# Stick-breaking attention inside an input projection: suffix sums with rounded fp32 operands in two parts, and another order of the step's matrix products

## What is computed

```python
z = einsum('bhqd,bhkd->bhqk', q, k) * scale
log_fail = where(before, log_sigmoid(-z), 0.0)          # before: key < query
later = cumsum(log_fail, axis=3, reverse=True) - log_fail
log_a = log_sigmoid(z) + later
a = where(before, exp(where(before, log_a, 0.0)), 0.0)
out = einsum('bhqk,bhkd->bhqd', a, v)
```

## Time and profile before

| | |
|---|---|
| median of 3 runs | 2329.61 us (2328.22 to 2335.32) |
| profiled execution, own time | 2328.99 us |
| its span, first to last instruction | 2327.3 us |
| PE busy | 2208.1 us, 95% |
| DVE, ACT, POOL busy | 1124.9, 855.8 and 417.6 us |
| mean granted TensorE clock | 0.964 |

### The profile page before, as it was taken

One profiled execution on the slowest core, in us unless ns is written; L12 is line 12 of the kernel. 1 busy time (PEld: TensorE's weight loads), 2 busy tenths in 40 slices (PEclk: granted clock), 3 DMA queues, 4 the chain that ended last, 5 costly groups with the idle time before them and its releaser, 6 DMA issues. The chain is left out here.

```text
span 2327.3 us, 29119 instructions
## 1 busy us (share of the span) xinstructions
PE 2208.1 (95%) x10778; PEld 1772.1 (76%) x10778; DVE 1124.9 (48%) x1810; ACT 855.8 (37%) x1407; POOL 417.6 (18%) x461
## 2 busy tenths in 40 slices
PE   7999999999889999998899989999999997999988
PEld 6888887766667888887788878886778887876657
DVE  5444324423436444324475544337656784655443
ACT  4322223443334322223432232135446743433453
POOL 2111002113333111001120010001100341014441
PEclk8999999999989999999899999999999997999999
DMA  4333333511022333331333246740243220242202
GB/s 136 115 92 98 93 100 84 95 46 55 19 73 73 108 91 99 91 99 52 103 98 90 82 76 108 98 80 1 73 119 82 55 55 20 76 97 60 52 19 67
DMA packets 359321, 182.10 MB, mean 78 GB/s; under 512 B 41926, under 2 KB 356015, under 8 KB 358831
## 3 DMA queue, kind: packets, MB, share of 16 engines
q1 hardware_dynamic: 359214, 180.69, 30.6%
HBM read 176.14 MB, written 4.52 MB: 78 GB/s over the span
## 5 line engine op out<-in xcount | busy, mean ns | idle before, releaser
L313 PE MATMUL ps<-xh,wh 128*128 128x512 f32 x1920 | 768.3, 400 | 12.9 <-DVE wl L280 10.9
L315 PE MATMUL ps<-xh,wl 128*128 128x512 f32 x1920 | 750.7, 391 | 0.0
L314 PE MATMUL ps<-xl,wh 128*128 128x512 f32 x1920 | 750.0, 391 | 0.0
L280 DVE TENSOR_TENSOR wl<-raw,wh 128x1024 fp32r<-128x1024 f32 x334 | 422.7, 1267 | 437.4 <-ACT wh L270 432.6
L270 ACT ACTIVATE wh<-raw 128x1024 fp32r<-128x1024 f32 x334 | 342.1, 1027 | 363.9 <-PE ps L315 332.6
L313 PEld LDWEIGHTS ps<-xh,wh 128*128 128x128 f32 x1920 | 361.9, 188 | 104.2 <-issue 18.2
L315 PEld LDWEIGHTS ps<-xh,wl 128*128 128x128 f32 x1920 | 361.6, 188 | 77.6
L314 PEld LDWEIGHTS ps<-xl,wh 128*128 128x128 f32 x1920 | 362.4, 189 | 73.6 <-issue 2.4
L457 PE MATMUL ps<-xh,wh 128*128 128x512 f32 x304 | 132.2, 435 | 26.2 <-ACT xh L392 15.5
L450 POOL TENSOR_TENSOR acc<-acc,sq 128x512 f32<-128x512 f32 x72 | 102.4, 1423 | 275.9 <-ACT sq L835 178.0
L314 PE MATMUL ps<-a_lo,wh 128*128 128x512 f32 x352 | 137.0, 389 | 0.0
(11 more groups left out here) (379 smaller groups left out, 2527.4 us busy)
## 6 DMA issues: line engine op xcount, KB each, us to landing
raw<-in_w_ffn_gate SPq DMA_DIRECT2D x44, 512.0 KB, 3.8
raw<-in_w_ffn_up SPq DMA_DIRECT2D x44, 512.0 KB, 3.8
raw<-in_w_ffn_down SPq DMA_DIRECT2D x32, 512.0 KB, 3.6
raw<-in_conv_w_in SPq DMA_DIRECT2D x32, 512.0 KB, 4.0
raw<-in_fox_w_in SPq DMA_DIRECT2D x32, 512.0 KB, 9.6
raw<-in_gdn_w_in SPq DMA_DIRECT2D x32, 512.0 KB, 4.1
raw<-in_w_in SPq DMA_DIRECT2D x24, 512.0 KB, 3.8
raw<-in_swa_w_in SPq DMA_DIRECT2D x32, 256.0 KB, 3.8
```

The source lines that it names most:

```text
L280: nc.vector.tensor_tensor(wl[s][:, 0:kb, :], raw[r][:, 0:kb, :], wh[s][:, 0:kb, :].bitcast(F32), ALU.subtract).then_inc(lo_done, 1)
L313: pe.matmul(o, wh[s][:, kb, :], x_hi, start=start, stop=False)
L314: pe.matmul(o, wh[s][:, kb, :], x_lo, start=False, stop=False)
L315: return pe.matmul(o, wl[s][:, kb, :], x_hi, start=False, stop=stop)
```

## The change

The softplus matrix is kept as two fp32r tensors, `softplus_hi` (rounded by ACT) and `softplus_lo` (the rest, by DVE), and `tri` becomes fp32r too. Each suffix product is then issued twice, once for each part. ACT's rounding comes after the exponential of the unit before; DVE's subtraction, `sb_rest`, stands ahead of the next step of the unit: within a tile right ahead of it, else at the start of the next tile that has a step, ahead of that tile's `wl`. On PE the sums over later blocks come first, once `sp_raw` says that z has been read, then the value product of unit s-2, and last the triangle, once the unit's own parts are there (`sp_parts`). `weights` gets two buffers of one unit each.

```diff
-            tri = sb("tri", [P, 2, P], ctx=c)
+            tri = sb("tri", [P, 2, P], F32R, ctx=c)
...
-            SP_ = sb("softplus", [P, 2, wide], ctx=c)
-            A = sb("weights", [P, 2, wide], ctx=c)
+            sp_hi = sb("softplus_hi", [P, 2, wide], F32R, ctx=c)
+            sp_lo = sb("softplus_lo", [P, 2, wide], F32R, ctx=c)
+            A = sb("weights", [P, 4, SEQ], ctx=c)
...
+            def sb_t(u, w):
+                return tmp[:, 2 * (u % 2):2 * (u % 2) + 2, 0:w]
+            def sb_a(u, w):
+                return A[:, 2 * (u % 2):2 * (u % 2) + 2, 0:w]
...
+                def suffix(u, k2):
+                    kb = sb_units[u][1]
+                    for r in range(2):
+                        for part in (sp_hi, sp_lo):
+                            m = pe.matmul(sb_z(u)[:, r, (k2 - kb) * P:SEQ - kb * P], ntri if k2 == kb else nones,
+                                          part[:, r, off[k2]:off[k2] + SEQ - k2 * P],
+                                          start=False, stop=True, skip_group_check=True)
+                    return m
                 if 1 <= s < SU + 1:
                     u = s - 1
-                    kb, z = sb_units[u][1], sb_z(u)
                     if u == 0:
                         pe.wait_ge(sbc, 2)
-                    pe.wait_ge(sp_d, u + 1)
-                    for r in range(2):
-                        for k2 in range(kb, TB):
-                            m = pe.matmul(z[:, r, (k2 - kb) * P:SEQ - kb * P], ntri if k2 == kb else nones,
-                                          SP_[:, r, off[k2]:off[k2] + SEQ - k2 * P],
-                                          start=False, stop=True, skip_group_check=True)
-                    m.then_inc(c_mm, 1)
+                    pe.wait_ge(sp_raw, u + 1)
+                    for k2 in range(TB - 1, sb_units[u][1], -1):
+                        suffix(u, k2)
                 if 2 <= s < SU + 2:
                     u = s - 2
                     pair, kb = sb_units[u]
...
                     pe.wait_ge(a_d, u + 1)
                     for r in range(2):
                         pe.matmul(ps[OUT][HD * r:HD * r + HD, kb * P:SEQ], v_cols(pair % 3, kb, r),
-                                  A[:, r, off[kb]:off[kb] + SEQ - kb * P],
+                                  sb_a(u, SEQ - kb * P)[:, r, :],
                                   start=kb == 3, stop=kb == 0, skip_group_check=True).then_inc(av_mm, 1)
+                if 1 <= s < SU + 1:
+                    u = s - 1
+                    pe.wait_ge(sp_parts, u + 1)
+                    suffix(u, sb_units[u][1]).then_inc(c_mm, 1)
...
-                    kb = sb_units[s][1]
-                    w = SEQ - kb * P
-                    dve.wait_ge(ln_d, s + 1)
-                    if s >= 4:
-                        dve.wait_ge(c_mm, s // 4 * 4)
-                    nc.vector.scalar_tensor_tensor(out=SP_[:, :, off[kb]:off[kb] + w], in0=sb_z(s),
-                                                   scalar=0.0, in1=tmp[:, 2 * (s % 2):2 * (s % 2) + 2, 0:w], op0=ALU.max,
+                    w = SEQ - sb_units[s][1] * P
+                    dve.wait_ge(ln_hi, ln_of(s))
+                    nc.vector.scalar_tensor_tensor(out=sb_t(s, w), in0=sb_z(s), scalar=0.0, in1=sb_t(s, w), op0=ALU.max,
                                                    op1=ALU.add).then_inc(sp_raw, 1)
+            def sb_rest(dve, u):
+                kb = sb_units[u][1]
+                w = SEQ - kb * P
+                o = off[kb]
+                dve.wait_ge(ln_hi, hi_of(u))
+                nc.vector.tensor_tensor(sp_lo[:, :, o:o + w], sb_t(u, w), sp_hi[:, :, o:o + w].bitcast(F32),
+                                        ALU.subtract).then_inc(sp_parts, 1)
+            def ln_of(u):
+                return 2 * u + 1
+            def hi_of(u):
+                return 2 * u + 2
...
-                    t = tmp[:, 2 * (s % 2):2 * (s % 2) + 2, 0:w]
+                    t = sb_t(s, w)
                     act.wait_ge(z_mm, 2 * s + 2)
                     if s >= 2:
-                        act.wait_ge(sp_raw, s - 1)
-                    nc.scalar.activation(t, sb_z(s), ACT.Abs).then_inc(abs_d, 1)
-                    act.wait_ge(abs_d, s + 1)
-                    nc.scalar.activation(t, t, ACT.Exp, scale=-1.0).then_inc(exp_d, 1)
-                    act.wait_ge(exp_d, s + 1)
-                    nc.scalar.activation(t, t, ACT.Ln, bias=1.0).then_inc(ln_d, 1)
+                        act.wait_ge(sp_parts, s - 1)
+                    nc.scalar.activation(t, sb_z(s), ACT.Abs).then_inc(abs_exp, 1)
+                    act.wait_ge(abs_exp, 2 * s + 1)
+                    nc.scalar.activation(t, t, ACT.Exp, scale=-1.0).then_inc(abs_exp, 1)
+                    act.wait_ge(abs_exp, 2 * s + 2)
+                    nc.scalar.activation(t, t, ACT.Ln, bias=1.0).then_inc(ln_hi, 1)
                 if 1 <= s < SU + 1:
                     u = s - 1
-                    kb = sb_units[u][1]
                     act.wait_ge(c_mm, u + 1)
-                    if u >= 4:
-                        act.wait_ge(av_mm, u // 4 * 8)
-                    nc.scalar.activation(A[:, :, off[kb]:off[kb] + SEQ - kb * P], sb_z(u), ACT.Exp).then_inc(a_raw, 1)
-
-            def sb_pool(pool, s):
-
+                    if u >= 2:
+                        act.wait_ge(av_mm, 2 * u - 2)
+                    nc.scalar.activation(sb_a(u, SEQ - sb_units[u][1] * P), sb_z(u), ACT.Exp).then_inc(a_raw, 1)
                 if s < SU:
                     kb = sb_units[s][1]
-                    v = SP_[:, :, off[kb]:off[kb] + P]
+                    act.wait_ge(sp_d, s + 1)
+                    if s >= 4:
+                        act.wait_ge(c_mm, s // 4 * 4)
+                    nc.scalar.activation(sp_hi[:, :, off[kb]:off[kb] + w], t, ACT.Copy).then_inc(ln_hi, 1)
...
+            def steps_of_sb(k):
+                return [s for kind, s in act_at(k) if kind == "s"]
+            def dve_between(dve, i, j, part):
+                at = steps_of_sb(4 * i + j)
+                if part == 1 and at and 1 <= at[0] < SU + 1:
+                    sb_rest(dve, at[0] - 1)
             def dve_amid(dve, k):
                 for kind, s in act_at(k):
+                    if kind == "s" and s != steps_of_sb(k)[0] and 1 <= s < SU + 1:
+                        sb_rest(dve, s - 1)
                     dve_do(dve, kind, s)
...
-                nc.gpsimd.memset(nones, -1.0).then_inc(sbc, 1)
+                nc.gpsimd.memset(nones.bitcast(F32), -1.0).then_inc(sbc, 1)
...
-            in_proj("mix_in", gains("g_mix_pre"), None, update=half[:, 0, :], evac_dve=mix_evac,
+            in_proj("mix_in", gains("g_mix_pre"), None, update=half[:, 0, :], evac_dve=mix_evac, between_dve=dve_between,
```

More of the change, by code:

```diff
@@ L1297, in kernel_program @@
                 "sq", "sum", "mm", "ms", "inv", "root", "spread", "rstd", "f"))
-            (sbc, z_mm, abs_d, exp_d, ln_d, sp_raw, sp_d, c_mm, a_raw, a_d, av_mm, o_d) = (sem(f"sb_{x}") for x in (
-                "const", "z", "abs", "exp", "ln", "spraw", "sp", "c", "araw", "a", "av", "o"))
+            (sbc, z_mm, abs_exp, ln_hi, sp_raw, sp_d, sp_parts, c_mm, a_raw, a_d, av_mm, o_d) = (sem(f"sb_{x}") for x in (
+                "const", "z", "absexp", "lnhi", "spraw", "sp", "parts", "c", "araw", "a", "av", "o"))
             ntri, nones = tri[:, 0, :], tri[:, 1, :]
@@ L1370, in sb_act @@
                     w = SEQ - sb_units[s][1] * P
-                    t = tmp[:, 2 * (s % 2):2 * (s % 2) + 2, 0:w]
+                    t = sb_t(s, w)
                     act.wait_ge(z_mm, 2 * s + 2)
                     if s >= 2:
-                        act.wait_ge(sp_raw, s - 1)
-                    nc.scalar.activation(t, sb_z(s), ACT.Abs).then_inc(abs_d, 1)
-                    act.wait_ge(abs_d, s + 1)
-                    nc.scalar.activation(t, t, ACT.Exp, scale=-1.0).then_inc(exp_d, 1)
-                    act.wait_ge(exp_d, s + 1)
-                    nc.scalar.activation(t, t, ACT.Ln, bias=1.0).then_inc(ln_d, 1)
+                        act.wait_ge(sp_parts, s - 1)
[4 more added lines that the diff above has]
+                    nc.scalar.activation(t, t, ACT.Ln, bias=1.0).then_inc(ln_hi, 1)
                 if 1 <= s < SU + 1:
                     u = s - 1
-                    kb = sb_units[u][1]
                     act.wait_ge(c_mm, u + 1)
-                    if u >= 4:
-                        act.wait_ge(av_mm, u // 4 * 8)
-                    nc.scalar.activation(A[:, :, off[kb]:off[kb] + SEQ - kb * P], sb_z(u), ACT.Exp).then_inc(a_raw, 1)
+                    if u >= 2:
+                        act.wait_ge(av_mm, 2 * u - 2)
+                    nc.scalar.activation(sb_a(u, SEQ - sb_units[u][1] * P), sb_z(u), ACT.Exp).then_inc(a_raw, 1)
+                if s < SU:
+                    kb = sb_units[s][1]
+                    act.wait_ge(sp_d, s + 1)
+                    if s >= 4:
+                        act.wait_ge(c_mm, s // 4 * 4)
```

(11 more changed lines are left out.)

## The result

The changed kernel takes 2316.36 us (median of 5 runs, 2314.38 to 2319.34), the kernel before in the same comparison 2329.74 us (5 runs, 2328.22 to 2335.32). The medians differ by 13.4 us; the ratio is 0.9945 with a 95% interval of 0.9935 to 0.9956, so 0.55% less. The forecast was 2318.0 us, 11.6 us less, in a range of 2314.5 to 2324.5. The profiled execution took 2315.31 us, its span is 2313.6 us.

What follows compares the result with a forecast made beforehand. PE's own work was taken to bound the sixteen units. 12.8 us saved on suffix records, less waits of 0.5, 0.4 and 0.3, gave 11.6 us off the 2329.61 median: 2318.0 us, stated range 2314.5 to 2324.5.

Steps and rivals of the forecast that it cites:

- Part 1: Suffix sums on PE: 160 records in fp32r instead of fp32, cheaper from 256 columns on, save 12.8 us.
- no gain below 512 columns: Bound on the suffix records: narrow fp32r products cost the same as fp32 records, leaving 3.2 us saved.
- the flat 0.11 up to 384 columns: Bound on the suffix records: 0.11 us each at 384 and 256 columns too, 15.2 us saved.
- second: Rival, suffix products: narrow fp32r products gain nothing; 3.2 us saved less 1.2, 2327.6 us; chance 0.05.
- third: Rival, suffix products: a narrow fp32r product costs a whole fp32 product of its width; 10.5 us slower, 2340; chance 0.05.
- fourth rival: Suffix products: narrow ones cost columns alone, 0.057 us at 128; 16.4 us saved less 1.2, 2314.4; chance 0.03.
- Part 2: New order on PE: same number of shape changes except in four steps; 0 to 0.4 us gained, taken as 0.
- Part 3: Sixteen roundings on ACT and subtractions on DVE fit in idle time; triangle waits for both, unit 11 cover 0.2 us.
- The two losses: PE waits: 0.5 us at unit 0's triangle, 0.4 us at the transposition behind step 2.
- The fifth rival: Time is given back behind the units, in the banded part or later; 2324 to 2329 us; chance 0.03.
- the longer chain: First rival: ACT, DVE and hand-overs take longer than walked, the triangle waits; 2321 or 2327 us; chance 0.10.

Runs made afterwards that it cites:

- the order alone: Kernel before with only PE's new order, all fp32 in one tensor, no roundings or subtractions: 2326.60 us against 2327.42, ratio 0.9997.
- the parts alone: Changed kernel with all suffix products of a unit behind the wait for `softplus_lo` and ahead of the value product: 2325.29 us, ratio 0.9985.
- the second comparison: Changed kernel run again, unaltered, against the kernel before: 2317.80 us against 2329.01, ratio 0.9956.

## Why the prediction was right

The time lay in the range and 1.6 us from the forecast, and the mechanism of the gain is the one described: PE's own work sets the pace of the units, the suffix records cost it less, and what is spared comes off the end. Term by term:

- *Part 1, 12.8 us forecast.* With 0.112, 0.120, 0.177 and 0.236 us a record, against 0.11, 0.12, 0.17 and 0.227 taken, the 160 records cost 22.4 us instead of 34.6: 12.2 us. Of the bounds around it, no gain below 512 columns (3.2 us) and the flat 0.11 up to 384 columns (15.2) are both excluded by rows, and with them the second, third and fourth rival. "Scaled by columns down to the floor of the loads" was the right reading; at 128 columns a record costs 0.112 us, twice what columns alone would, and that is the distance of two loads in the earlier trace rows. An fp32r record costs 0.55 of the fp32 record of its width at 256, 384 and 512 columns, and as much as that record at 128. The Trainium skill ("FP8 and Floating Point Precision", TensorE Precision Notes) gives true FP32 four passes, which alone would make it one half at every width and the saving 17.3 us. The trace comes within a tenth of that from 256 columns on and not at 128, where 3.6 of the 5.1 us between 17.3 and 12.2 lie.
- *Part 2, nothing forecast.* With everything in fp32 the order gave 0.5 us, a little above the bound of 0.4. With the parts it is worth more: PE's own work is 118.0 us in the old order and 116.7 in the new, 1.3 us. So the part on the order was too low, and PE's own work fell by 13.1 us in all and not by the 12.2 of the record prices.
- *Part 3, the triangle.* The walk for unit 11 put the triangle's turn 9.4 us behind the score product of that unit and its parts at 9.2. In the trace the triangle starts 9.47 behind it (495.72 to 505.19) and the subtraction, the DVE row below, ends at 8.82. Cover 0.66 instead of 0.2, so this unit doesn't wait. The other tight ones: 0.78 for unit 10 (0.9 forecast), 0.35 for unit 15 (0.3), 0.28 for unit 3 (about 0). The 0.3 us of waits set aside for units 3, 11 and 15 didn't come.
- *The two losses.* Unit 0 waited 0.43 us (0.5 forecast), the transposition behind step 2 0.45 more than before (0.4).
- *What was missing: 2.05 us.* The step that failed is the sentence that ACT's and DVE's new work "costs nothing where PE has other work", followed by the triangle alone as the one that waits for both. I walked what waits for the new instructions and not what is queued behind them. The copy to `F` is, behind `wl`; and the part on the order counted changes of shape without asking what else the value product lost when it went ahead of the triangle. It takes both: the order alone makes no such wait, the parts alone make one of 0.3 us at each of the two steps, and together it is 1.02.

The sum: 13.1 - 0.43 - 0.45 - 2.05 = 10.2 us, as measured in the units. The forecast was 11.6, by 12.8 - 1.2. The medians of the whole differ by 13.4 us, and by 11.2 in the second comparison. That the forecast lies between the two is luck in part: the missing wait of 2.05 us was offset by what lies outside the units, 3.0 us behind them in the first pair of profiles and 0.6 in the second, and 0.5 and 0.7 ahead of them. Whether 1 us or so of the 11.2 to 13.4 is still the change's, outside the units, the runs leave open.

The fifth rival, time given back behind the units, fell: nothing was given back. The first, the longer chain, was not at work in the changed kernel, but it is close: without the early sums PE waits 7.0 us for the same parts instead of 0.4.

Contention, two engines that slow each other down, is the remaining point. Timeline of the changed kernel beside units 10 and 11, DVE and then POOL:

```profile
497.62 2.30 DVE L280 TENSOR_TENSOR wl<-raw,wh 128x1024 fp32r<-128x1024 f32 x1
...
503.31 1.23 DVE L1386 TENSOR_TENSOR softplus_lo<-softplus_parts,softplus_hi 128x1024 fp32r<-128x1024 f32 x1 [1.61 <-ACT softplus_hi L1418]
```

```profile
496.96 1.87 POOL L1580 TENSOR_TENSOR out_square_sums<-out_squares 128x512 f32<-128x512 f32 x1
```

Unit 11's subtraction ran alone and took 1.23 us, not 1.36. But the `wl` ahead of it, pushed back by unit 10's subtraction, met POOL's sum of squares and took 2.30 us against 1.23 alone. The Trainium skill ("GPSIMD Engine Reference", Key points) names this contention of GpSimd with DVE instructions that have two SBUF inputs; the trace agrees in kind, with 1.07 us in one instruction, eight times the 0.13 of the earlier trace rows. In these traces the engine that started later pays: here `wl` ends 1.09 us behind the end of POOL's operation, a little less than its length alone. In the kernel before, the same `wl` started 0.29 us ahead of the end of a mask of POOL and took 0.13 us longer; the product of squares that POOL then started beside it took 2.01 us, against 1.04 for the same one alone here (POOL's spans are rough). The 1.07 us cost nothing only because the softplus sum behind it started later still, at 500.48.

## What to carry to other kernels

When an instruction is put into an engine's queue, walk two lists: who waits for it, and what stands behind it and who waits for that; here the first list was right to 0.5 us at the four tight units and the second, not walked, cost 2.0 of 12 us. When a product is moved earlier on PE, what frees its bank loses cover by the same amount (here the turn came 0.84 us earlier, counted from the score product), so check the evacuation, not only the operands. Measure a gain of 10 us in 2300 between two fixed points of the trace that enclose the change (here good to 0.1 us), and repeat the unchanged kernel before you explain what the whole time shows beyond that.

## What I had not expected of the hardware

- The first fp32r product of a group costs 0 to 0.1 us more: 0.05 at 128 columns behind a score product, nothing at 384 behind 256 columns, 0.1 behind a value product from 256 columns on.
- At 128 columns one fp32r record costs 0.112 us, as much as one of the two fp32 records, so two rounded parts save nothing there.
- A DVE subtraction of 1024 elements that started beside a running POOL operation took 2.30 us instead of 1.23.
- The same 1776 us of work behind the units took 1776.2 to 1785.0 us, with 136.5 to 157.0 us at the lower clock, in kernels that don't differ there.
